# Chunk 0 of two feed-forwards by plain products instead of Strassen-Winograd, with x normalised on VectorE

## The reference

```
x = x + 0.5 * swiglu(rmsnorm(x, g_ffn1), w1_gate, w1_up, w1_down)
mix, ... = token_mix(rmsnorm(x, g_mix), ...)          # pooling mixer and SSD mixer
x = x + mix
x = x + cross_attn(rmsnorm(x, g_xq), k_mem, v_mem, w_xq, w_xo)
x = x + 0.5 * swiglu(rmsnorm(x, g_ffn2), w2_gate, w2_up, w2_down)
y = rmsnorm(x, g_final)

def swiglu(h, w_gate, w_up, w_down):
    return (jax.nn.silu(h @ w_gate) * (h @ w_up)) @ w_down
def rmsnorm(x, g):
    y = xf * lax.rsqrt(jnp.mean(xf * xf, axis=-1, keepdims=True) + EPS)
    return (y * g.astype(jnp.float32)).astype(x.dtype)
```

## Time and profile before

| | us |
|---|---|
| runs, median (lowest, highest) of 3 | 2420.02 (2418.61, 2420.3) |
| profiled execution, own time | 2421.36 |
| its span | 2419.4 |
| PE busy | 2247.1 (93%) |
| DVE busy | 1455.1 (60%) |
| ACT busy | 672.5 (28%) |
| POOL busy | 425.6 (18%) |

### The profile page before, as it was taken

One profiled execution on the slowest core, in us unless ns is written; L12 is line 12 of the kernel. 1 busy time (PEld: TensorE's weight loads), 2 busy tenths in 40 slices (PEclk: granted clock), 3 DMA queues, 4 the chain that ended last, 5 costly groups with the idle time before them and its releaser, 6 DMA issues.

```text
span 2419.4 us, 41583 instructions
## 1 busy us (share of the span) xinstructions
PE 2247.1 (93%) x16140; PEld 2171.3 (90%) x16140; DVE 1455.1 (60%) x2643; ACT 672.5 (28%) x1112; POOL 425.6 (18%) x366
## 2 busy tenths in 40 slices
PE   4599999998999899999999999985999999989998
PEld 4499999998999899996899987985999999989998
DVE  5865555654666776546877335268655556556666
ACT  4322222221112333144723134032222222212112
POOL 6321111213122000002310000071211112132120
PEclk7799999999999999999999999997999999999999
DMA  4123131224223221127723334311231313142321
GB/s 160 60 63 96 57 101 53 83 66 172 100 80 114 91 59 54 37 81 230 236 96 124 122 107 156 124 72 39 66 93 57 101 53 92 58 174 98 106 70 72
DMA packets 222555, 234.29 MB, mean 97 GB/s; under 512 B 8963, under 2 KB 179729, under 8 KB 222185
## 3 DMA queue, kind: packets, MB, share of 16 engines
q1 hardware_dynamic: 222449, 232.83, 29.5%
HBM read 180.42 MB, written 52.48 MB: 96 GB/s over the span
## 4 chain that ended last, share of the span: by engine, by line
PE 46%; DVE 6%; issue 5%; DMA 3%; POOL 2%; ACT 1%; DVEq 0%; SPq 0%; ACTq 0%; POOLq 0%
PE bank L2791 12%; PE bank L2793 12%; PE bank L2792 12%; DMA w_raw<-in_w_up_dram 2%; DVE w_lo L1804 1%; PE bank L3399 1%; POOL act L1001 1%; PE bank L3411 1%; ACT w_hi L1206 1%; PE bank L3513 1%; PE bank L3431 1%; PE bank L3290 1%; PE bank L3294 1%; PE bank L3228 1%; DMA act_keep<-act 0%
## 5 line engine op out<-in xcount | busy, mean ns | idle before, releaser
L2791 PE MATMUL bank<-h_hi,w_hi 128*128 128x352 f32 (+1 forms) x3376 | 1053.2, 312 | 93.2 <-DVE h_lo L1825 23.0
L2792 PE MATMUL bank<-h_lo,w_hi 128*128 128x352 f32 (+1 forms) x3376 | 1040.2, 308 | 0.0
L2793 PE MATMUL bank<-h_hi,w_lo 128*128 128x352 f32 (+1 forms) x3376 | 1040.1, 308 | 0.0
L2791 PEld LDWEIGHTS bank<-h_hi,w_hi 128*128 128x128 f32 x3376 | 644.1, 191 | 103.4 <-issue 69.5
L2792 PEld LDWEIGHTS bank<-h_lo,w_hi 128*128 128x128 f32 x3376 | 645.5, 191 | 0.0
L2793 PEld LDWEIGHTS bank<-h_hi,w_lo 128*128 128x128 f32 x3376 | 643.8, 191 | 0.0
L1963 DVE SCALAR_TENSOR_TENSOR x<-bank,x 128x352 f32<-128x352 f32 x528 | 271.3, 523 | 189.9 <-PE bank L2793 189.9
L1804 DVE TENSOR_TENSOR w_lo<-w_raw,w_hi 128x1024 fp32r<-128x1024 f32 x132 | 182.4, 1396 | 106.9 <-ACT w_hi L1206 106.4
L2792 PE MATMUL bank<-xr,w_hi 128*128 128x264 f32 x704 | 199.9, 284 | 0.0
L2793 PE MATMUL bank<-xr,w_lo 128*128 128x264 f32 x704 | 199.6, 284 | 0.0
L2791 PE MATMUL bank<-xr,w_hi 128*128 128x264 f32 x704 | 199.6, 283 | 0.0
(11 more groups left out here) (399 smaller groups left out, 2915.6 us busy)
## 6 DMA issues: line engine op xcount, KB each, us to landing
act_keep<-act SPq DMA_DIRECT2D x88, 264.0 KB, 2.1
w_raw<-in_w_gate_dram SPq DMA_DIRECT2D x44, 512.0 KB, 4.9
w_raw<-in_w_up_dram SPq DMA_DIRECT2D x44, 512.0 KB, 5.6
w_raw<-in_w_down_dram SPq DMA_DIRECT2D x44, 512.0 KB, 3.6
h_raw<-act_keep SPq DMA_DIRECT2D x24, 528.0 KB, 4.6
l_raw<-act_keep SPq DMA_DIRECT2D x20, 528.0 KB, 5.3
w_raw<-in_w_in_dram SPq DMA_DIRECT2D x18, 512.0 KB, 3.9
x<-x_keep SPq DMA_DIRECT2D x6, 1408.0 KB, 10.3
```

The source lines that it names most:

```text
L2791: eng.matmul(out, a_hi, b_hi, start=first, stop=False, skip_group_check=onto)
L2792: eng.matmul(out, a_hi, b_lo, start=False, stop=False, skip_group_check=onto)
L2793: return eng.matmul(out, a_lo, b_hi, start=False, stop=last, skip_group_check=onto)
```

## The change

Chunk 0 of both feed-forwards is no longer made by Winograd but by six plain pairs (PAIRS: block fi, tile n), each of GATE and UP, 8 k tiles by three matmuls of 352 columns, 48 matmuls, 288 in all. Strassen's sums of x are made for chunk 1, which is written out by hand (first_chunk); the loop is `Fori(2, LAST)`. x is normalised on VectorE, one instruction for a k tile of 352 columns (x_scale), with ACT's high and VectorE's low part tile by tile (x_split). GpSimd now makes the norm factors of the second and third group of row tiles (x_stats). Activation products move to VectorE (times, in up_sums), the store of quarter (0,0) has its own semaphore s_act11. In the loop take_w of GATE stands before the second set of weight lows and sums, ACT does its silus before the weight splits. The down phase has six banks up to chunk 8 (sum_bank), starts after mixing step "12" of GATE and (for m = 2) of UP, and the last two chunks' 12 matmuls for a tile and block go to one bank (pair_down) with one add (pair_add); in the second feed-forward for n = 0, 1 alone. mid_hi9, mid_lo9 are buffers of their own for chunk 9 of the first one. The core of the diff (of the two first_chunk, the one with s1_s3 is VectorE's, the one with s2_split ACT's):

```
+PAIRS = ((0, 0), (1, 0), (0, 1), (1, 1), (0, 2), (1, 2))
-X_GROUPS = ((0, 1, 2), (3, 4), (5, 6, 7, 8))
+X_GROUPS = ((0, 1, 2), (3, 4, 5), (6, 7, 8))
...
+            def plain_pair(f, j, between=None):
+                fi, n = PAIRS[j]
+                if f and j == 1:
+                    eng.wait_ge(p_free, 126)
+                if j >= 2:
+                    eng.wait_ge(g_mix, plain_mixed(f, j - 2))
+                def step(m, k):
+                    if k == 0:
+                        eng.wait_ge(g_rdy, plain_ready(f, fi, m))
+                    eng.wait_ge(o_lo, 28 * f + KT * n + k + 1)
+                    slot, ks = g_slot("AC"[fi], m), slice(k * P, (k + 1) * P)
+                    return three(plain_bank(f, j, m)[:, 0:TN], w_hi[:, slot, ks], w_lo[:, slot, ks], h_hi[:, k, cols(n)],
+                                 h_lo[:, k, cols(n)], k == 0, k == KT - 1)
+                if j == 0:
+                    last = [[step(m, k) for m in range(2)] for k in range(KT)][-1]
...
+            def x_scale(f, n, k):
...
+                xk = x[:, k, cols(n)]
+                eng.scalar_tensor_tensor(out=xk, in0=xk, scalar=par[:, g:g + 1], in1=rb[:, cols(n)], op0=ALU.mult,
+                                         op1=ALU.mult).then_inc(o_sum, 1)
...
+            def first_chunk(f):
+                plain_mult(f, 3)
+                s1_s3(f)
+                plain_mult(f, 4)
+                s2_s4(f)
+                for m in range(2):
+                    g_low(f, 1, "A", m)
+                    sums_13(f, 1, m)
+                sums_24(f, 1, GATE)
+                s2_s4_low(f)
+                for kind in "DB":
+                    g_low(f, 1, kind, GATE)
+                plain_mult(f, 5)
+                s1_low(f)
+                s3_low(f)
+                for t in range(2):
+                    act_11(f, 1, t)
...
+            def first_chunk(f):
+                for m in range(2):
+                    g_hi(f, 1, "A", m)
+                s2_split(f)
+                s4_split(f)
+                for kind in "DB":
+                    g_hi(f, 1, kind, GATE)
+                plain_act(f, 5)
+                take_p1(f, 1, GATE, 0)
+                s1_split(f)
+                take_p1(f, 1, GATE, 1)
+                s3_split(f)
...
+            def up_sums(f, c, between=None):
+                for j, step in enumerate((take_u, take_21, take_12)):
+                    for t in range(2):
                         step(f, c, UP, t)
+                    for t in range(2):
+                        times(f, c, j, t)
...
+            def plain_mixed(f, j):
+                return len(MIX) * chunks(f, 0) + (len(MIX) if j == 5 else j + 1)
...
+            def sum_bank(i):
+                return bank[(0, 1, 2, 4, 5, 7)[i % 6]]
...
+            def pair_down(f, n, between=None):
...
+                    out = (sum_bank, down_bank)[f](KT * n + m)[:, 0:TN]
+                    ms = slice(m * P, (m + 1) * P)
+                    for c, parity in ((LAST - 1, 1), (LAST, 0)):
+                        for fi in range(2):
...
+                    mm.then_inc(f_d, 2)
```

More of the change, by code:

```diff
@@ L992, in multiply @@
-            def multiply(f, c):
-                n = chunks(f, c)
-                for j, (half, fi, step) in enumerate(((1, 1, "22"), (1, 0, "21"), (0, 1, "12"))):
-                    eng.wait_ge(g_evict, evicted(f, c, "silu", GATE, j))
-                    for t in range(2):
-                        u_ = (p522[t][:, :], first_p[UP][:, t, :], wsum[:, t, :])[j]
-                        eng.wait_ge(g_mix, mixed(f, c, step, UP, t))
-                        out = quarter(act, half, fi, t)
-                        eng.tensor_tensor(out, u_, out, ALU.mult).then_inc(g_act, 1)
@@ L1246, in silu_11 @@
             def silu_11(f, c, t):
[L1248 removed]
+                wait(eng, s_act11, 16 * chunks(f, c))
                 eng.wait_ge(g_prod, done(f, c, GATE, 2, t))
@@ new lines, in x_low, with x_split @@
+            def x_low(f, n, k):
+                eng.wait_ge(o_hi, 28 * f + KT * n + k + 1)
+                eng.tensor_tensor(h_lo[:, k, cols(n)], x[:, k, cols(n)], h_hi[:, k, cols(n)].bitcast(F32), ALU.subtract)\
+                   .then_inc(o_lo, 1)
+            def x_split(f, n, between=None):
+                for k in range(KT + 1):
+                    if k < KT:
+                        x_scale(f, n, k)
+                    if k:
+                        x_low(f, n, k - 1)
+                    if between is not None:
+                        between(k)
@@ new lines, in strassen_chunk, with strassen_rest @@
+            def strassen_chunk(f, c):
+                g_low(f, c, "C", UP)
+                for t in range(2):
+                    act_11(f, c, t)
+                strassen_rest(f, c)
+            def strassen_rest(f, c):
+                g_low(f, c + 1, "A", GATE)
+                sums_13(f, c + 1, GATE)
+                for t in range(2):
+                    take_w(f, c, GATE, t)
+                g_low(f, c + 1, "A", UP)
+                sums_13(f, c + 1, UP)
+                gate_sums(f, c)
+                sums_24(f, c + 1, GATE)
+                for t in range(2):
+                    take_w(f, c, UP, t)
@@ L2877, in product @@
-                if (m, p) == (UP, 1) and before:
+                if first and t == 0 and m == GATE and p in (3, 5, 6, 7):
+                    eng.wait_ge(o_lo, 28 * f + {6: 25, 3: 26, 5: 27, 7: 28}[p])
+                if first and t == 0 and (m, p) == (GATE, 1):
+                    eng.wait_ge(g_mix, plain_mixed(f, 4))
+                if (m, p) == (UP, 1):
                     eng.wait_ge(g_mix, mixed(f, c, "12", UP, t) - len(MIX))
-                elif p == 4 and before:
+                elif p == 4:
```

784 lines of the change are left out of this document (406 added, 378 removed).

## The result

The changed kernel takes 2314.38 us (median of 4 runs, 2311.78 to 2316.32) where the kernel before takes 2420.16 (4 runs): the ratio is 0.956, 95% interval 0.9543 to 0.9577. Forecast was 2310, range 2290 to 2335. The profiled execution took 2316.32, its span 2314.6, which is 104.8 less than 2419.4.

A forecast was written before the change was run, and what follows sets the result against it. TensorE, nearly always busy, bounds it, through needless work and idle or half-clock stretches. Openings 40.6 and 29.4, loop 22.6, chunk 10 3.4, down starts 10.8, shared banks 3.3 and 0.3 sum to 110.4 us: forecast 2310, range 2290 to 2335.

The forecast's parts named there:

- where the pairs of the first opening were said to wait: First chunk 0: pair 1 waits for tile 1's x (38.5 us), pairs 3 to 5 for the last group (near 58).
- rival E: Openings: x transfers of tiles 1 and 2 land late, each lost 6 us costing +10, 2330 us; chance 0.09.
- the very copy named: Chunk 1: ACT's copy of Winograd's first GATE product, waiting for pair 5's product, idles TensorE from 84.2 to 93.1 us.
- The rival that chunk 1's chain would be hidden: Chunk 1, both feed-forwards: ACT and VectorE work during pair 5, the 9 us idles vanish, 2292 us; chance 0.17.
- The 4.9 us: Chunk 0: six plain pairs take 45.8 us against 40.9 for Winograd, +4.9 in each feed-forward if all were covered.
- a semaphore of its own for quarter (0,0) takes that hold away: Loop: SiLU, held by the act_keep transfer, delays ACT's p_up copy; TensorE's wait of 4.1 us in 8 turns goes.
- rival A: Loop: VectorE's queue, with 2.6 us more work, brings TensorE's waits back, 2332 us; chance 0.11.
- Forecast 2.2 and a half-clock part: Down starts: wait of 6.5 us falls to about 2.2, half-clock cost from 3.4 to 1.7; 5.4 gained each.
- The term of 3.3: Last two down chunks, first feed-forward: shared banks drop 24 adds, 61.6 us becomes 58.3, gaining 3.3.
- rival C: Down phases: shared banks and the new down start give nothing, waits only change place, +14, 2324 us; chance 0.08.
- a change of +0.3 for the pairs: Second feed-forward's last two down chunks: sharing banks, with 16 adds fewer, gains 0.3 us.
- The rule against it: First opening: 14 small GpSimd statistics steps each wait out a VectorE instruction, 7.7 us; pair 1 or 2 some 3 later, 2313.

The follow-up runs named there:

- the old order: Changed kernel with the loop of the kernel before, but quarter (0,0) keeping its own store semaphore: 2347.1 us, 41.90 us a turn.
- the whole old loop: Changed kernel with GpSimd products, one condition for four stores, take_w late, ACT's old order and VectorE's old UP order: 2358.2 us, ratio 0.9741.
- the four tried alone: Single edits to the changed kernel: products on GpSimd 2329.6 us, one condition for four stores 2315.5, take_w late 2324.2, ACT's order old 2315.0.
- The fifth: VectorE's old loop order, UP take_u ahead of the next chunk's lows; not run alone against the changed kernel, so no time of its own.

## Why the prediction was right

The time was 4 us above the forecast, and each of the nine stages but one, the shared banks', lies within 2.5 us of its own. Most of them came as reasoned. In two places the reasoning failed though the stage came out right: where the pairs of the first opening were said to wait, and the semaphore in the loop.

*Openings.* First matmul at 25.1 (forecast 24.5). Pair 0 ends at 34.2 (35). Pair 1 starts at 38.3 (38), but not for the reason given. The prediction has pair 1 wait for x of tile 1 and pairs 3 to 5 for the last group; by PAIRS, though, pair 1 is of tile 0 and pair 3 of tile 1. The trace says the same, as pair 1 runs before the first scale of tile 1:

```profile
37.59 1.10 PE L2952 MATMUL bank<-diag,ones 128*128 128x128 f32 x6 [3.27 <-POOL diag L997]
38.34 0.64 PE L2913 MATMUL bank<-h_hi,w_hi 128*128 128x352 f32 x1
...
39.91 1.08 DVE L1849 SCALAR_TENSOR_TENSOR x<-x,par,rb 128x352 f32<-128x352 f32 x2 [0.63 <-DMA x_keep<-x]
```

TensorE's queue has the spread of the second group's factors in front of pair 1, and that waited for GpSimd's diagonal. So 38 was right by luck. x_keep landed later than forecast (VectorE gets it at 39.9 and 62.9; forecast 38.5 and 58), but TensorE ran pair 1 while the store of tile 1's x was awaited, and pair 3 while tile 2's was, so rival E did not come. Three pairs at 0.160 us a matmul end at 84.3 (81.3): 3 us late, as pairs 1 and 2, with transposes and small waits for lows among them, held pair 3 until 61.3 (58.4). Then the idle: 8.5 us from 87.1, forecast 8.9 from 84.2, ended by the very copy named, behind the very product named (94.5, forecast 92.7). Chunk 2 starts at 136.8, forecast 136: chunk 1 took 52.5 us and not 54.7, which makes up for most of the late chunk 0. In the second opening the pairs took 48.9 us (49.2). The rival that chunk 1's chain would be hidden (2292) is refuted for the change as made, though the run with pair 5's product early shows that part of it can be.

*Plain products.* 144 matmuls in 23.0 us are 0.160 each, where the sum used 0.159. The 4.9 us that they cost over Winograd's are small against what chunk 0 lost, 101.2 us to 59.3. But no run separates plain products from scaling x on VectorE, GpSimd's lighter part and the new order of the first transfers: a chunk 0 by Winograd with x scaled on VectorE was not tried, so how much of the 39.8 and 28.5 us of the two openings, two thirds of the whole gain, belongs to the plain products is open.

*Loop.* The size was right (11.6 and 11.0 forecast, 13.4 and about 12.9 measured), the mechanism half wrong. The step "a semaphore of its own for quarter (0,0) takes that hold away" failed as a cause: with one condition for all four stores put back alone, the turn stays the same, and even in the old order the semaphore gives 0.37 to 0.43 us of the 0.5 to 0.8 expected before that run. The hold was real (and 3.92 us again in the whole old loop), but with VectorE's and ACT's new orders the last products are finished 2.5 us earlier against the copy, and TensorE no longer feels it. take_w's place is real, 0.46 us a turn. The VectorE multiplies were hidden as said, and rival A (2332) did not come: neither loop wait is left.

*Down starts.* Forecast 2.2 and a half-clock part, measured 2.35 and 3.4 us at half clock behind it; down chunks 0 to 8 gained 5.4, as forecast, with a spread of 1.8 us between traces. The run with GpSimd's products shows that this is what moving them is worth (5.5). The other reason given, that the banks ask only for "12", shortened nothing in that run.

*Shared banks.* The term of 3.3 came to nothing: -1.0 in this trace, 0.2 by the average of the traces with the same code there. For this term rival C was right. The wait for chunk 10's lows was put at 4.2 and was 5.4, as the two lows took 4.80 instead of 2.44; and the end of the phase pushed its adds and the splits behind it into the projections, where the first 144 matmuls took 28.9 us instead of 25.8. I had ended the stage too early. The run with chunk 10's lows early shows the wait's part in it: 3.1 to 3.4 us of each down phase come back. In the second feed-forward I had charged a change of +0.3 for the pairs and forgotten that the same 5.4 us stand there: 3.6 gained instead of 5.7.

*The middle*, not changed, took 2.3 us more at a clock of 0.99. Both profiles have 6.8 us at half clock there (from 1149.4 before, from 1089.5 after); the changed kernel's has 3.4 more, from 1041.8. What set them off I cannot say. The twelve other traces, with the same code in the middle, take 698.2 to 700.9 us, so the 2.3 are spread and not an effect of the change.

*The rule against it.* The Trainium skill, page "SBUF — State Buffer", section "SBUF: two separate sides", says that a VectorE operation with two SBUF inputs and a GpSimd operation that reads SBUF shut each other out of the port they share for a whole instruction. On GpSimd's side this trace agrees. The small steps of the statistics of group 1, of 0.20 us alone, beside VectorE's instructions:

```profile
32.83 0.19 POOL L991 TENSOR_TENSOR nrm<-nrm 128x3 f32<-128x3 f32 x1
33.10 1.14 POOL L992 TENSOR_TENSOR nrm<-nrm 128x3 f32<-128x3 f32 x1
34.33 1.05 POOL L993 TENSOR_SCALAR nrm<-nrm 128x3 f32<-128x3 f32 x1
35.46 0.19 POOL L994 TENSOR_TENSOR nrm<-nrm 128x3 f32<-128x3 f32 x1
35.76 1.77 POOL L997 TENSOR_SCALAR diag<-ident,nrm 128x128 f32<-128x128 f32 x3
```

The two long ones run beside two weight lows of 1.2 us each (2.35 us for the two, from 32.98). The whole took 8.9 us, from 28.6 to 37.5, where 14 undisturbed steps at 0.28 from start to start and three diagonals make about 5.7; TensorE waited 3.3 for it. Undisturbed, an estimate from these rows puts the end of the diagonals at 34.3, as pair 0 ended, and the wait at next to nothing. So the cost that the prediction gave to the rule, 3 us at pair 1, was there, and the sum without it had pair 1 at the right time by the wrong premise on tile 1. That the statistics on VectorE would be faster was not tried.

## What to carry to other kernels

Where the operands of a phase are late at its start, doing its first unit by the dearer, simpler algorithm can pay by taking the preparation off the path: with 4.9 us more work, and the scaling moved to VectorE in the same change, the first opening gained 40. Follow the queue of the helper engine past the place you changed: the preparation comes back at the next unit, and the first thing that waits there is often not the late operand but a cheap instruction (here a copy) tied to a counter that a late one raises; moving that one gave a half to a third of the idle back. When a loop is freed by several edits, undo each alone and all together: here three of the four tried alone cost the loop nothing, one cost 0.46 us a turn, and all five together 1.5. The fifth should have been undone alone too. And compare a stage with other traces of the same code before giving its 2 us a cause.

## What the hardware showed that I had not expected

Two weight lows of VectorE beside GpSimd's splits of mid took 4.80 us, 2.40 each instead of 1.22. And a gap of 2.35 us was followed by 3.4 us at half clock while a longer one, 3.6 us in front of pair 1, was followed by 3.4 as well, and the two of 8.5 us by 10.2 in the first opening and 6.8 in the second. In the run with one condition for the four stores, the same gap of 2.35 us (idle 2.03 in both rows) at the same place had none behind it: the clock was 1.00 from 508.2 to 515.0, where the changed kernel had 0.50 from 509.3 to 512.7. Idle of the same length did not cost the same each time.
